# Turning an expert's token rows by VectorE in 32x32 blocks instead of by TensorE, in a two-layer hybrid step with a mixture of experts

## The reference, cut to what matters

```python
def _hier_moe(h, p):
    gl = (h @ p['w_group_router'])                       # best group of 4
    el = (h @ p['w_expert_router']).reshape(B, S, N_GROUPS, EXPERTS_PER_GROUP)
    top_v, top_i = lax.top_k(el_sel, TOP_K)              # best 2 of its 4 experts
    top_w = jax.nn.softmax(top_v, axis=-1) * g_p[..., None]
    ...
    for gi in range(N_GROUPS):
        a = jnp.einsum('bsd,edf->bsef', h, p['w_e1'][gi])    # D 1024 -> F 512
        b = jnp.einsum('bsd,edf->bsef', h, p['w_e3'][gi])
        y = y + jnp.einsum('bsef,efd->bsd', jax.nn.silu(a) * b * w_all[:, :, gi, :, None], p['w_e2'][gi])
    return y
```

## Time and profile before

| | us |
|---|---|
| median of 3 runs | 2040.04 |
| lowest and highest | 2034.2, 2041.99 |
| the profiled execution | 2054.78 |
| its span | 2053.0 |
| TensorE busy | 1966.6 |
| VectorE busy | 698.5 |
| ScalarE busy | 473.6 |
| expert part of layer 0 (first hidden to last project) | 760.8 to 1052 |
| expert part of layer 1 | 1739.3 to 2030 |

### The profile page before, as it was taken

One profiled execution on the slowest core, in us unless ns is written; L12 is line 12 of the kernel. 1 busy time (PEld: TensorE's weight loads), 2 busy tenths in 40 slices (PEclk: granted clock), 3 DMA queues, 4 the chain that ended last, 5 costly groups with the idle time before them and its releaser, 6 DMA issues.

```text
span 2053.0 us, 29144 instructions
## 1 busy us (share of the span) xinstructions
PE 1966.6 (96%) x12526; PEld 1064.7 (52%) x12526; DVE 698.5 (34%) x1669; ACT 473.6 (23%) x926; POOL 98.6 (5%) x135
## 2 busy tenths in 40 slices
PE   6989999999999989999989999999999998999996
PEld 3444556656655544444445565665665554444443
DVE  1293366333311131222223956633331113122223
ACT  2301234344200131011133133334420002111112
POOL 0000100100000010000020010010000001000002
PEclk9999999999999989999999999999999999999998
DMA  9777671321222549999952223132213243999993
GB/s 400 250 292 271 218 261 46 111 108 62 89 96 102 205 159 349 390 393 393 396 205 110 86 89 128 46 106 96 79 62 123 103 202 147 349 391 391 390 399 124
DMA packets 45168, 421.67 MB, mean 205 GB/s; under 512 B 5888, under 2 KB 6032, under 8 KB 18928
## 3 DMA queue, kind: packets, MB, share of 16 engines
q1 hardware_dynamic: 30240, 369.43, 46.5%
q0 software_dynamic: 8080, 26.78, 3.8%
q10 hardware_dynamic: 6720, 23.60, 3.2%
HBM read 389.08 MB, written 28.61 MB: 203 GB/s over the span
## 4 chain that ended last, share of the span: by engine, by line
PE 86%; DMA 8%; ACT 1%; DVE 1%; another core or an unknown queue 1%; issue 1%; POOL 1%; SPq 0%; POOLq 0%; ACTq 0%; DVEq 0%
PE psum L988 16%; PE psum L734 16%; PE psum L1092 9%; PE psum L1003 8%; PE psum L737 6%; PE psum L1113 6%; DMA pc<-we_in 5%; PE psum L1097 5%; PE psum L1034 4%; DMA ring<-wmod_in 2%; PE psum L652 2%; PE psum L828 2%; DMA ring<-wch_in 1%; PE psum L712 1%; PE psum L1108 1%
## 5 line engine op out<-in xcount | busy, mean ns | idle before, releaser
L734 PE MATMUL psum<-hT,ring 128*128 128x384 f32 x1088 | 367.2, 491 | 2.0 <-ACT pc L1270 1.9
L988 PE MATMUL psum<-hT,ring 128*128 128x384 f32 x1024 | 343.2, 488 | 0.0
L734 PEld LDWEIGHTS psum<-hT,ring 128*128 128x128 f32 x1088 | 203.0, 191 | 145.6 <-issue 18.7
L988 PEld LDWEIGHTS psum<-hT,ring 128*128 128x128 f32 x1024 | 192.1, 190 | 130.6
L1003 PE MATMUL psum<-pc,ring 128*128 128x384 f32 x512 | 175.6, 486 | 0.0
L2119 DVE TENSOR_TENSOR ytok<-pc,psum 128x384 f32<-128x384 f32 x32 | 17.7, 554 | 342.7 <-ACT pc L1525 342.7
L2111 DVE COPY scr<-psum 64x512 f32<-64x512 f32 (+1 forms) x180 | 91.9, 510 | 114.8 <-PE psum L1113 113.2
L1003 PEld LDWEIGHTS psum<-pc,ring 128*128 128x128 f32 x512 | 95.4, 190 | 61.5
L1720 DVE SCALAR_TENSOR_TENSOR pc<-pc,par 128x384 f32<-128x384 f32 x240 | 127.2, 611 | 0.0
L737 PE MATMUL psum<-ring,hT 128*128 128x512 f32 x288 | 125.8, 594 | 0.0
L1937 DVE TENSOR_TENSOR mva<-mva,psum 128x384 f32<-128x384 f32 x48 | 26.6, 554 | 282.4 <-PE psum L1003 263.4
(11 more groups left out here) (338 smaller groups left out, 2022.0 us busy)
## 6 DMA issues: line engine op xcount, KB each, us to landing
ring<-we_in SPq DMA_DIRECT2D x48, 2048.0 KB, 18.5
pc<-we_in SPq DMA_DIRECT2D x48, 2048.0 KB, 18.9
ring<-wmod_in SPq DMA_DIRECT2D x42, 1024.0 KB, 5.9
ring<-wch_in SPq DMA_DIRECT2D x18, 2048.0 KB, 8.6
ring<-wgate_in SPq DMA_DIRECT2D x16, 2048.0 KB, 8.1
ring<-wbr_in SPq DMA_DIRECT2D x16, 1024.0 KB, 8.0
ring<-wtok_in SPq DMA_DIRECT2D x6, 2048.0 KB, 8.3
expert_out_rows<-scr ACTq DMA_DIRECT2D x30, 384.0 KB, 9.5
```

Source lines behind the costliest of these rows:

```text
L734: mm = pe.matmul(F[:, 0:T], wv[:, k, n * P:(n + 1) * P], hT[:, k, :], start=k == 0, stop=k == KD - 1)
L988: mm = pe.matmul(bank(5 + n % 2)[:, 0:T], wv[:, k, (n % 4) * P:(n % 4 + 1) * P], hT[:, k, :], start=k == 0, stop=k == KD - 1)
```

## The change

`x_rows` becomes 128 partitions by 768 values. `load_rows(e)` is now four DMAs instead of one: DMA q brings the q-th quarter (256 values, 1 KB) of all 96 rows into the 32 partitions from 32q on, three rows to a partition. One VectorE instruction then turns all 32x32 blocks of that and writes `x_h` directly. So that the features come out in the places that `hidden` expects, `htok` is stored with its features permuted (`htok_k`): ScalarE's copies write it, and the pick of expert 0's rows reads it, with a step of 8 values (32 bytes).

```diff
-        x_rows = [mva_flat[0:CAP, 512:1536], pc_flat[0:CAP, 12288:13312]]
+        x_rows = [mva_flat[:, 512:1280], pc_flat[:, 12288:13056]]
+        htok_k = htok.rearrange("p t (n k) -> p t k n", k=KD)
...
-                def turn_rows(e):
-                    pe.wait_ge(rows_in[e % 2].sem, rows_in[e % 2].at(l, (e + 1) // 2 * 16))
-                    for k in range(KD):
-                        mm = pe.transpose(x_turned[:, k, :], x_rows[e % 2][:, k * P:(k + 1) * P], ident[0:CAP, 0:CAP])
-                    mm.then_inc(xt_done.sem, 1)
...
-                        mm = pe.matmul(x_turned[:, k, :], htok[:, t, k * P:(k + 1) * P], first_pick[:, t * P:t * P + CAP],
+                        mm = pe.matmul(x_turned[:, k, :], htok_k[:, t, k], first_pick[:, t * P:t * P + CAP],
...
                 for e in range(NE - 1):
                     hidden(e)
-                    turn_rows(e + 1)
                     if e >= 1:
                         project(e - 1, 0)
...
-                    ac.activation(htok[:, t, half * W:(half + 1) * W], bank(n), ACT.Copy).then_inc(ht_copied.sem, 1)
-
-                def copy_rows(e):
-                    ac.wait_ge(xt_done.sem, xt_done.at(l, e + 1))
-                    ac.activation(x_h, x_turned, ACT.Copy).then_inc(xh_ready.sem, 1)
...
+                    ac.activation(htok_k[:, t, half * 4:half * 4 + 4],
+                                  bank(n).rearrange("p (k n) -> p k n", k=4), ACT.Copy)\
+                      .then_inc(ht_copied.sem, 1)
...
                 def load_rows(e):
-                    ac.dma_start(x_rows[e % 2], xs_d[e * CAP:(e + 1) * CAP, :]).then_inc(rows_in[e % 2].sem, 16)
+                    src = xs_d[e * CAP:(e + 1) * CAP, :].rearrange("(b i) n -> i b n", b=CAP // SUB)
+                    for q in range(P // SUB):
+                        ac.dma_start(x_rows[e % 2][SUB * q:SUB * q + SUB, :].rearrange("i (b c) -> i b c", b=CAP // SUB),
+                                     src[:, :, q * 256:(q + 1) * 256]).then_inc(rows_in[e % 2].sem, 16)
...
                     ac.activation(x_s, x_ab[:, :, 0, :], ACT.Silu).then_inc(xs_ready.sem, 1)
-                    if e + 1 < NE:
-                        copy_rows(e + 1)
                     if e < NE - 3:
+                        ac.wait_ge(xh_ready.sem, xh_ready.at(l, e + 2))
                         load_rows(e + 3)
...
+                def turn_rows(e):
+                    ve.wait_ge(rows_in[e % 2].sem, rows_in[e % 2].at(l, (e + 1) // 2 * 64))
+                    ve.wait_ge(xab_done.sem, xab_done.at(l, e))
+                    ve.transpose(x_h.rearrange("p k (b i) -> p b k i", b=CAP // SUB),
+                                 x_rows[e % 2].rearrange("p (b j k) -> p b k j", b=CAP // SUB, k=KD))\
+                      .then_inc(xh_ready.sem, 1)
...
                 for e in range(NE - 1):
+                    turn_rows(e + 1)
                     open_hidden(e)
                     if e >= 1:
                         keep_out(e - 1)
```

7 lines of the change are left out of this document (4 added, 3 removed).

## The result

The median is 2071.18 us (2069.39 to 2073.16, 4 runs) against 2040.43 us (2034.2 to 2041.99, 4 runs) before: a ratio of 1.0149 with a 95% interval of 1.013 to 1.0169, 30.7 us or 1.5% slower. The forecast was 11.9 us. So the sign is sure, and the size is 20 to 31 us. The profiled execution took 2072.35 us, its span is 2070.6 us.

A forecast was written before the change was run, and what follows sets the result against it. DMA bounds the expert loop, 18.2 us an expert against TensorE's 17.35. Turns -1.46, quarter loads +5.2 and pick +2.2 make +5.9 us a layer, +11.9 for both, on 2040.0: 2052 us, range 2020 to 2078.

The forecast's parts named there:

- What bounds the loop: Expert loop: DMA is slower, 18.2 us an expert against TensorE's 17.35; turns removed survive as only -1.46 us a layer.
- the quarter loads: Row loads of experts 3 to 15: 13 loads, each 0.4 us dearer in full DMA engines, +5.2 us a layer.
- d: Extra DMA time of one row load after the change: +0.4 us taken, bounds -0.08 and 1.3.
- 13 d: Shift of hidden(14)'s start, counted from the end of hidden(0): from 229.0 us to about 234.
- The observable: ScalarE's DMA queue q10: packets between two experts rise from 224 to about 304, share from 12.6% to about 15%.
- The pick: TensorE's pick of expert 0's rows, weights read with a 32-byte step: +2.2 us a layer, between 0 and 4.4.
- VectorE's reduce: Evidence for the pick's upper bound: a 128-byte step costs VectorE +0.72 ns a value, giving 4.4 us.
- ScalarE: Loses a copy, gains three DMA issues and a wait; stepped htok copies take about 1 us of cover at most: 0.
- VectorE's turn: Turn of 768 values in the expert loop: 0.88 to 1.43 us, even 2.9 us hidden under 5.4 us of cover: 0.
- Expert 0: Without a project as cover, hidden(1) starts 0.9 us later; DMA stays fed, so cost 0.
- The rule on ports: Loads into 32 neighbouring partitions reach 8 of 16 ports, so half speed; judged little borne out by a 22% dearer transfer.
- the third rival: Row loads cost about double: d = 1.1 gives +30 us, 2070 us; d = 1.3 gives 2075; chance 0.12.

The follow-up runs named there:

- e9: Changed kernel with unstepped pick, gate product ahead of VectorE's turn, and row loads on GpSimd's queue; 2055.74 against 2054.5 us for the kernel before, ratio 1.0007.
- e7: Kernel before with its 4 KB rows loaded by three DMAs of 32 neighbouring partitions each; 2072.89 against 2057.78 us, ratio 1.0083.
- e1: Kernel before with its row load cut into four DMAs of 96 partitions by 1 KB, TensorE's turns kept; 2036.76 against 2039.47 us, ratio 0.9977.
- e2: Changed kernel with rows loaded by one DMA of 128 partitions by 3 KB, wrong rows turned; 3351.95 us, ratio 1.643, another branch ran; loops 533.9 us.
- e5: Changed kernel with its four row loads issued on GpSimd's queue instead of ScalarE's; 2066.85 against 2057.78 us for the kernel before, ratio 1.0039.
- e3: Changed kernel with htok in natural order, the pick without steps, input weights permuted instead; 2057.45 against 2039.47 us for the kernel before, ratio 1.0074.
- e4: Changed kernel with the gate product ahead of the next expert's turn on VectorE; 2073.68 against 2057.78 us for the kernel before, ratio 1.0084.
- e6: Changed kernel with a third buffer for loaded rows, each load issued one expert earlier; 2069.41 against 2057.78 us for the kernel before, ratio 1.0062.
- e8: Changed kernel, unchanged, run again beside the kernel before on one chip; 2074.94 against 2054.5 us, ratio 1.0094.
- e11: Kernel before with rows loaded in four DMAs of 96 partitions by 256 columns, repeated on another chip; 2047.81 against 2054.5 us, ratio 0.9973.

## Why the prediction was wrong in size and right in sign

**What bounds the loop: right for the kernel before, taken too far for the changed one.** The DMA's 18.2 us an expert against TensorE's 17.35 is what the kernel before shows. The change took 0.81 us an expert from TensorE (period 16.53 us wherever nothing waits), and none of it reached the end. e9 shows it with the pick, the order and the queue put right: 15 turns a layer removed, ratio 1.0007. But the 18.2 us are no fixed pace of the DMA. They go with the form of the rows' load: 19.0 with 32 partitions (e7), 17.5 or less with 1 KB pieces into 96 (e1), 16.7 or less with 3 KB pieces into 128 (e2), where the turns do pay.

**The step that failed: the quarter loads priced as their own engine time only, with the weights as what is late.** The prediction counted a load as 112 packets today and 192 after the change, "if a partition's three pieces go as one packet", priced them at d = +0.4 us of DMA engine time, and let hidden(14) move by 13 d. Three things in that term were wrong. The number that it gave for the loop was near by luck: +9.1 us forecast between hidden(1) and (14) in both layers, +12.8 measured, though the waits for `we_in` that it was made of, some 16 us a layer, are not there at all.

First, the count. q10 has 16800 packets in the whole run where before it had 6720, so a load is 448: every 1 KB piece goes by itself, 384 of them and 64 completions. The observable was 304 packets of q10 between two experts; 4270 / 7.77 are 550.

Second, the price. It was put together from the load's own packets, and the weights' 16.0 us an expert were held fixed. But these move with the rows beside them: q1's share times 140 us, for 6.29 of its MB, is 14.8 us in e2, 15.5 in e1, 16.7 in e7. So the term has two parts of opposite sign. 1 KB pieces speed the DMA up (e1: 17.5 us an expert, 0.7 less), 32 neighbouring partitions slow it down (e7: 19.0, 0.8 more). In the changed kernel they seem to cancel nearly: 18.0 us an expert, though with fewer rows in it (5.90 MB on q10 are 1.9 transfers an expert, before 2.1). e5 and e9, with the same loads in larger packets, have 18.4, so d is 0.2 there and not 0.4. q10's share is 12.5%, not the 15% forecast. In e2 d would be -1.5, far outside the bounds of -0.08 and 1.3.

Third, and this is the mechanism: the prediction never asked *which queue* a full DMA makes late. It took the weights for the late one, as before, and called the rows harmless since they are asked for two experts ahead. Here are q1 and q10 over the same 35 us (845 to 880, two periods and a little), first in the kernel before, then in the changed one:

```profile
q1 hardware_dynamic: 837, 12.19, 87.7%
q10 hardware_dynamic: 456, 1.61, 12.6%
```

```profile
q1 hardware_dynamic: 872, 12.71, 91.3%
q10 hardware_dynamic: 871, 1.16, 9.4%
```

872 against 871: the two queues get the same number of packets. e3 has 866 and 866, e4 877 and 879, e6 876 and 876, e8 876 and 878. A weight packet carries 16 KB, a row packet 1 KB. An expert needs 432 packets of q1 (three blocks, 128 pieces and 16 completions each) and 560 of q10 (448 for the load, 112 for the store). As long as q1 always has work, q10 gets only 432 of its 560 an expert. In the kernel before it needs 224 and the question doesn't arise. In e1 it needs 560 too and got 1120 against q1's 867 in the same stretch: TensorE's turns keep the period at 17.34 us, the weights are landed after 15.2, and q10 has the engines to itself in the rest. So it takes both parts of the change to starve the rows much: packets sixteen times smaller than the neighbour's, and a TensorE fast enough to keep the neighbour's queue full. With the small packets alone TensorE waited for rows once in each trace, 0.5 us (e1) and 3.2 (e11). With the fast TensorE and 144 packets of 3 KB a load, 256 of q10 an expert, nothing waited (e2). The Trainium skill, page "DMA: Bandwidth & Descriptors", section "Queues, rings and completion order", says that a DMA engine goes round its queues packet by packet; by that rule the counts agree, 872 and 871.

When rows come late, TensorE stops while the weights run ahead: the second block that hidden(14) of layer 0 needs lands 5.9 us before its start, in the kernel before 0.65. In one place of layer 0 the DMA stops too, which I take for full rooms. Windows of the changed kernel: us, busy of PE, PEld, DVE, ACT, POOL, PE clock, DMA share, GB/s.

```profile
906.70:915.10 8.40, 8.40 (x33) 2.53 (x32) 3.06 (x6) 0.49 (x1) 0.00 (x0) 0.83 1.02 394
...
965.00:980.00 15.00, 11.99 (x95) 4.86 (x99) 5.17 (x8) 0.49 (x1) 0.00 (x0) 0.80 0.83 312
980.00:995.00 15.00, 15.00 (x127) 5.56 (x123) 5.19 (x8) 0.98 (x2) 0.00 (x0) 1.00 0.91 344
```

The first row is the hidden behind the gap at its lower clock. In the other two the DMA share falls to 0.83 and 0.91, where the kernel before has 1.00 and 1.01. (0.17 + 0.09) x 15 = 3.9 us of it are idle there. From the end of hidden(0) (781.28) to hidden(14) (1019.48) it is 238.2 us, forecast 234 and before 229.0: +9.2 instead of +5.2 - 0.65. The idle DMA's 3.9 us is of the size of the 4.65 us between, but it is not shown to be the same time, and it is no general account: over the whole of these 238.2 us the DMA share is 0.99 (before 1.00), and in e8, whose loops sum to the same, it is 1.00. There the engines are full all the time and no hidden waits for weights, so part of what they bring is not needed yet.

What undoing it gives: e2, fewer packets on the same queue and all partitions, both at once, loops 38.6 us shorter; e5, fewer packets on another queue, 8.5 us shorter, ratio 1.0039. e6, the same packets asked for one expert earlier, has loops 11.1 us shorter, ratio 1.0062, with the waits moved to the stores. So the late rows come with the number of packets, since e5 keeps the partitions and e2 the queue; how the 38.6 us divide between packets and partitions no run separates.

**The pick: right in kind, half its size.** Forecast +2.2 us a layer with 4.4 as the upper bound. Layer 0's pick, its loads of weights before and after, with the shortest, median and longest in ns, and ScalarE's copies after:

```profile
L1130 PEld LDWEIGHTS psum<-mod_rows,vals x48: 192/192/333, 750.9 to 758.0; 128*128 128x128 f32 x48
...
L1125 PEld LDWEIGHTS psum<-mod_rows,vals x48: 312/335/338, 755.2 to 766.4; 128*128 128x128 f32 x48
...
L1493 ACT ACTIVATE vals<-psum 128x512 f32<-128x512 f32 x12 | 11.8, 1125 | 3.1 <-PE psum L1054 3.1
```

The pick takes 11.71 us instead of 7.46: +4.25 us, near the 4.4 that VectorE's reduce had given. I took the middle of the two bounds without a reason. But the upper one came true by luck, for most of the 4.25 us is not shown to be the step's. Before, the pick begins at the lower level, 1.2 GHz (0.50), with 213 ns from one matmul to the next and 333 ns a load of weights. From 754.9 us on it runs at 2.4 GHz, and the last 30 of the 48 matmuls come every 112 ns. In the changed kernel all 48 run at 0.50, with 238 ns each and 335 a load. At the same level the step costs 25 ns a matmul, 1.2 us in all. The other 3.0 us are the 30 matmuls that stayed at the lower clock. What the step costs at 2.4 GHz, and why the clock stayed low, no run shows; e3, without the step, is back at 213 and then 112 ns. The windows of the pick and of the hidden(0) behind it in layer 0, columns as above:

```profile
755.30:767.00 11.70, 11.70 (x50) 11.70 (x51) 5.11 (x28) 0.00 (x0) 5.96 (x6) 0.50 0.63 249
768.30:777.70 9.40, 9.40 (x36) 2.77 (x40) 0.00 (x0) 1.28 (x1) 0.00 (x0) 0.75 0.31 85
```

Beyond the sum: in layer 0 the granted clock is 0.50 during the pick and 0.75 in the hidden(0) behind it, which takes 9.42 us; before, it was 0.73 and 0.81, and hidden(0) took 8.78 us. In layer 1 hidden(0) takes 8.66 us instead of 7.09. That puts 2.2 us on top of both layers. By the Trainium skill's note on cachelines (page "SBUF — State Buffer", section "Door 1: The DMA port swizzle") steps beyond 16 bytes are slower; the trace agrees in direction for TensorE, 238 against 213 ns at the same clock, and by far less than VectorE's row.

**ScalarE: 0, right.** Its copies into `htok` take 1125 ns instead of 591 with the same step, a price that nobody on the path pays by any row here.

**VectorE's turn: 0 for its length, right; but its place was not free.** 1574 ns, a little over the 1.43 us of the higher row. The prediction checked who waits when the turn is *long*, and found 5.4 us of cover. It didn't ask who is queued behind it when its rows are *late*: the gate product, and behind that turn_hidden. What this order is worth is open: e4's loops are 4.3 us shorter in layer 0 and 0.3 in layer 1, and the medians, 1.0084 and 1.0094 on different chips, can't tell it.

**Expert 0: the later start right, the 0 wrong.** Forecast was a hidden(1) 0.9 us later and no cost. Hidden(0) to (1) grew by 1.6 and 2.5 us. Of that 0.6 and 1.6 are the slower hidden(0) of the pick's paragraph; the 0.9 left in each layer is the turn (in e4 and e9 hidden(1) waits 0.93 us for it). How much of it the fed DMA absorbs further on, no run separates.

**The rule on ports.** The prediction kept it as the third rival with 0.12, whose 2070 us is nearly what was measured, though not by its mechanism: its price was half speed for each quarter load, d = 1.1. e7 measures the 32 neighbouring partitions alone: 0.8 us a load on a base of 1.08, and a ratio of 1.0083 for the whole kernel. By the rule of the Trainium skill ("SBUF — State Buffer", "Door 1: The DMA port swizzle") such a load has half the ports; e7 agrees in direction, and most of the way in size. The row that I weighed it against was a quiet transfer, with no weights beside it, and only 22% dearer; e7's loss is in the weights beside the rows. In the changed kernel the small pieces seem to give the price back, and in e2, where all 128 partitions are reached by one DMA, the loop is fast.

**In sum,** over both layers, forecast and the profiled loops, by the table's columns:

| | forecast | measured |
|---|---|---|
| pick to hidden(0) | +4.4 | +7.2 |
| hidden(0) to (1) | 0 | +4.1 |
| hidden(1) to (14) | +10.4 - 1.3 | +12.8 |
| hidden(14) to (15) | -1.6 | +0.8 |
| together | +11.9 | +25.0 |

Of the 13.1 us that the sum lacks, 2.8 are the pick, 4.1 expert 0's hidden, 3.7 the waits up to hidden(14) and 2.4 the last period, which in layer 0 shrank by 0.8 us as forecast and in layer 1 held a hidden(14) of 9.48 us, the slowed one from above. The medians say +20 and +31. Why these two differ is open: the two profiles of the changed kernel agree within 0.3 us in the loops, and not in the stretches outside, which the change hardly touches.

## What to carry to other kernels

When the DMA engines are full, count packets for each queue before costing bytes: a queue of small packets beside one of large packets gets as many turns, not as many bytes, and it starves just when the other queue never runs dry. Making the compute engine faster can be what keeps it from running dry. Price a transfer by what its neighbours take beside it too, not by its own packets alone: beside the same 384 KB of rows the weights took 14.8 us an expert of the engines' time in one form (128 partitions, 3 KB, e2) and 16.7 in another (32 partitions, e7). Then ask, for each wait that the change moves to another engine, what is queued behind it there, since a late transfer stops that too. And when the total of a run means nothing, as in e2, a stretch of its trace may still answer the question.

## What the hardware showed that I had not expected

- On ScalarE's queue each 1 KB piece was a packet by itself (448 for four loads), on GpSimd's the same loads took far fewer: e5's q0 has 384 packets for 0.79 MB between 845 and 880 us, two loads, so 192 each: the 128 that were the first guess for ScalarE's queue, and 64 completions.
- Smaller packets beside 16 KB ones made the total faster: 404 GB/s in e1 and 406 in e11, against 393 and 391 in the two profiles of before. Why, no run here tells.
- Loads into 32 neighbouring partitions slow the weights of the other queue, while their own queue's share stays at 12.5% (e7). One load over 128 partitions in 3 KB pieces leaves them faster than any other form here: 425 GB/s in all, weights at 52.63 MB in 140 us against 48.37 before (e2).
- The same kernel before had medians of 2039.5, 2054.5 and 2057.8 us on three chips, 0.9% apart; where two profiles could be compared, the difference lay outside the expert loops.
